# Feed-forward first products of groups 1 to 3 as seven half-size products (Strassen-Winograd) instead of eight, with VectorE summing the weight tiles

## What the kernel computes

```python
def _squared_relu_mlp(x, w1, w2):      # w1: 1024 x 4096, w2: 4096 x 1024
    h = jax.nn.relu(x @ w1)
    return (h * h) @ w2
```

## Time and profile before

| | |
|---|---|
| median of three runs | 2035.89 us |
| the profiled execution: span, which is all that its record gives of its time | 2036.2 us |
| TensorE busy with matmuls | 2016.6 us (99%), clock granted in full |
| VectorE busy | 1043.6 us (51%) |
| ScalarE busy | 803.1 us (39%) |
| DMA | 182.14 MB, 89 GB/s on average |

### The profile page before, as it was taken

The page is one execution under the profiler, slowest core; times in us unless marked ns, Lnnn a source line. Parts: engine busy times, 40 slices in busy tenths (PEclk is TensorE's granted clock), DMA queues, the critical chain, the costliest instruction groups (busy, mean ns, idle before and its releaser), DMA issues.

```text
span 2036.2 us, 27767 instructions
## 1 busy us (share of the span) xinstructions
PE 2016.6 (99%) x11212; PEld 1707.4 (84%) x11212; DVE 1043.6 (51%) x1722; ACT 803.1 (39%) x1354; POOL 174.5 (9%) x162
## 2 busy tenths in 40 slices
PE   9999999999999999999999999999999999999998
PEld 7888898888889888889888888987888898888887
DVE  6657777344345636537443434738544545334344
ACT  6425654232233533324332323535544345223232
POOL 1001010100002002210210003300000220000000
PEclk9999999999999999999999999999999999999999
DMA  5222012232322322222323223232122313332321
GB/s 189 83 73 74 22 53 92 95 104 92 103 83 94 124 93 83 83 94 83 104 86 111 82 93 104 94 104 94 53 63 83 99 52 98 103 104 84 112 83 52
DMA packets 52002, 182.14 MB, mean 89 GB/s; under 512 B 5824, under 2 KB 8016, under 8 KB 51888
## 3 DMA queue, kind: packets, MB, share of 16 engines
q1 hardware_dynamic: 50064, 173.23, 26.6%
q0 software_dynamic: 1824, 7.32, 1.1%
HBM read 178.43 MB, written 2.10 MB: 89 GB/s over the span
## 4 chain that ended last, share of the span: by engine, by line
PE 93%; DVE 3%; ACT 2%; issue 1%; DMA 1%; POOL 0%; SPq 0%; ACTq 0%; DVEq 0%
PE ps L411 60%; PE ps L1126 5%; PE ps L492 4%; PE ps L531 3%; PE ps L1789 3%; PE ps L1866 3%; PE ps L1066 2%; PE ps L1109 2%; PE ps L1083 1%; PE ps L1488 1%; PE ps L1879 1%; PE ps L847 1%; PE ps L1625 1%; PE ps L1777 1%; PE ps L1833 1%; PE ps L1743 1%
## 5 line engine op out<-in xcount | busy, mean ns | idle before, releaser
L411 PE MATMUL ps<-xa,ring 128*128 128x512 f32 x3048 | 702.6, 391 | 0.0
L411 PEld LDWEIGHTS ps<-xa,ring 128*128 128x128 f32 x3048 | 570.4, 188 | 119.6 <-issue 2.0
L411 PE MATMUL ps<-xb,ring 128*128 128x512 f32 x2208 | 502.6, 389 | 0.0
L411 PEld LDWEIGHTS ps<-xb,ring 128*128 128x128 f32 x2208 | 414.5, 188 | 86.0
L384 DVE TENSOR_TENSOR ring<-raw,ring 128x1024 fp32r<-128x1024 f32 x320 | 403.8, 1267 | 161.5 <-ACT ring L376 160.7
L376 ACT ACTIVATE ring<-raw 128x1024 fp32r<-128x1024 f32 x320 | 334.9, 1053 | 300.3 <-DMA raw<-in_stream 300.2
L989 DVE TENSOR_TENSOR acc<-acc,ps 128x512 f32<-128x512 f32 x68 | 46.8, 688 | 222.5 <-PE ps L411 222.5
L972 DVE TENSOR_TENSOR ffsq<-relu 128x512 f32<-128x512 f32 x96 | 66.4, 692 | 181.7 <-ACT relu L931 181.7
L931 ACT ACTIVATE relu<-ps 128x512 f32<-128x512 f32 x64 | 38.2, 596 | 227.7 <-PE ps L411 225.4
L975 DVE TENSOR_TENSOR xb<-ffsq,xb 128x512 fp32r<-128x512 f32 x96 | 66.5, 693 | 75.8 <-ACT xb L923 75.8
L1126 PE MATMUL ps<-xa,ring 128*128 128x512 f32 x432 | 104.3, 396 | 0.0
(11 more groups left out here) (368 smaller groups left out, 2055.5 us busy)
## 6 DMA issues: line engine op xcount, KB each, us to landing
raw<-in_stream SPq DMA_DIRECT2D x320, 512.0 KB, 3.5
t<-in_rpb POOLq DMA_DIRECT2D x8, 384.0 KB, 4.8
h<-in_x SPq DMA_DIRECT2D x8, 256.0 KB, 6.8
c_w<-in_cmp_w POOLq DMA_DIRECT2D x4, 512.0 KB, 4.7
out_y<-h SPq DMA_DIRECT2D x10, 128.0 KB, 1.9
out_y<-h SPq DMA_DIRECT2D x3, 256.0 KB, 2.2
cons<-in_con SPq DMA_DIRECT2D x1, 578.0 KB, 8.8
raw<-in_stream SPq DMA_DIRECT2D x2, 256.0 KB, 3.9
```

The lines of the kernel that those rows point to most:

```text
L411: mm = nc.tensor.matmul(bank[:, :], ring[:, slot_of(n, looped), w, k * P:(k + 1) * P], operand[:, k, xx], start=(start and i == 0 and w == ...
```

## The change

Let a 1024x1024 part of w1 act on all 512 tokens. It is cut in two halves of 512 hidden channels (u = 0, 1). In each half the weights are a 2x2 arrangement of tiles ("11", "12", "21", "22": rows are output channels, columns input channels, each tile 256 outputs by 512 inputs, stored as 128x1024), and the input is a 2x2 arrangement of 512 channels by 256 tokens. Eight products of tile by quarter become seven (Winograd's form of Strassen's method): the tile used is sometimes a sum of tiles, and the quarter used is sometimes a mix of quarters. One product is 2 x 4 blocks x 3 matmuls, 24 matmuls of 256 columns.

What is done for it, in groups 1 to 3 of each feed-forward:

- TensorE: `pe_set`, seven products for each half, 336 matmuls of 256 columns a group. Five PSUM results are combined, two accumulate into earlier banks.
- VectorE: four sums of weight tiles (128x1024, `dve_add_tile`) for each half before the split, seven splits, five sums of 128x512 results (`dve_set_sums`, `dve_set_22`, `dve_set_12`, `dve_set_21`) and four low parts (`dve_quad_lo`). It no longer squares the relu.
- ScalarE: seven splits for each half, a copy out of PSUM (`act_set_a`), and for each of four quarters a relu and two squares (`act_quad`; with a bias the relu is two instructions).
- DMA: seven landings for each half (the four tiles, some of them loaded twice) and one more of tile "21" into `other`.
- Splits run two products ahead inside the sets, three before them.
- The first panel of the second product takes its blocks in the order (0,1), (4,5), (2,3), (6,7), each pair after its own low parts.
- Once per feed-forward, in the second product of group 0: four mixes of quarters (`dve_mixed_raw`, 16 VectorE instructions of 128x256), their high parts on ScalarE, their low parts on VectorE (4 of 128x1024), and four ScalarE copies of 128x256. The squares of `h` move to panels 7 to 10, two a panel.
- The hardware loops are written out. The means' matmuls move from the head of the last group into group 2, `pool_base_sum` runs before `pool_squares(pool, 2)`, and several semaphores are shared (a semaphore's name and count change, not what waits for what).
- Two VectorE instructions of 128x8 near the start of the kernel make `minus`, the negated gains.

The core of the diff:

```diff
+SET_LANDS = ("11", "22", "11", "12", "11", "12", "22")
+SET_ADDS = (None, "21", 1, 2, "21", None, None)
+SET_SUM = (None, 1, 2, 3, 4, None, None)
+SET_TURN = (0, 1, 2, 4, 3, 5, 6)
+SET_BANK = (0, 2, 1, 3, 1, 0, 3)
...
         def dve_split(dve, n):
             m = n + AHEAD
...
+            if m + 1 < NP and summed(m + 1) is not None:
+                dve_add_tile(dve, m + 1)
+            dve.wait_ge(hi_done, m + 1)
+            at = set_of(m)
+            if at is not None and at[1] in SET_ADDS:
+                dve.wait_ge(sem("set_sums"), summed(m + 1))
             nc.vector.tensor_tensor(ring[:, at_slot, 1], raw[:, at_slot, 1], ring[:, at_slot, 0].bitcast(F32),
                                     ALU.subtract).then_inc(lo_done, 1)
...
+        def dve_add_tile(dve, n):
+            d, i = set_of(n)
+            dve.wait_ge(landed[n % RING], 16 * (n // RING + 1))
+            if SET_ADDS[i] == "21":
+                dve.wait_ge(sem(f"other_in{d % 2}"), 16 * (d // 2 + 1))
+                more = other[:, d % 2]
+            else:
+                dve.wait_ge(sem("set_sums"), summed(n - i + SET_ADDS[i]))
+                more = raw[:, SLOT[n - i + SET_ADDS[i]], 1]
+            nc.vector.tensor_tensor(raw[:, SLOT[n], 1], raw[:, SLOT[n], 1], more, ALU.add).then_inc(sem("set_sums"), 1)
...
+        def pe_set(pe, s, g, u):
+            first, d = set_at(s, g, u)
+            for c in range(SEVEN):
+                n = first + SET_TURN[c]
+                bank = ps[BANK[n]]
+                if c < 4:
+                    pe_free_bank(pe, BANK[n], first)
...
+                if c == 4:
+                    pe.wait_ge(sem("set_sum"), 5 * d + 1)
+                if c == 5:
+                    pe.wait_ge(sem("set_act"), 9 * d + 1)
+                if c == 6:
+                    pe.wait_ge(sem("set_sum"), 5 * d + 3)
+                pe.wait_ge(lo_done, n + 1)
+                moving = set_moving(c)
+                for i in range(2):
+                    for k in range(4):
+                        for w, xx in ((0, 0), (0, 1), (1, 0)):
+                            at_w = (4 * i + k) * P
+                            mm = nc.tensor.matmul(bank[:, half(i)], ring[:, SLOT[n], w, at_w:at_w + P], moving[:, k, xx],
+                                                  start=(c < 5 and i == 0 and k == 0 and w == 0 and xx == 0),
+                                                  stop=(i == 1 and k == 3 and w == 1),
+                                                  skip_group_check=c >= 5)
+                mm.then_inc(panel_done, 1)
...
+            for g in range(1, GROUPS):
+                pe_set(pe, s, g, 0)
+                pe_set(pe, s, g, 1)
+                for k in range(KC if g < GROUPS - 1 else KC - 4):
+                    n = base + second_of(g) + k
+                    if k == 0:
+                        for i, (pair, quads_in) in enumerate((((0, 1), 3), ((4, 5), 4), ((2, 3), 7), ((6, 7), 8))):
+                            pe.wait_ge(sem("ff_lo"), u0 + KC * g + quads_in)
+                            pe_panel(pe, n, xb, blocks=pair, free=i == 0, split=i == 0, start=i == 0, stop=i == 3, last=i == 3)
...
+        def ffn_splits(s, g, j):
+            n = BASE[s] + first_of(g) + j
+            if g == 0:
+                ahead = (3,) if j >= 4 else ()
+            elif j < 2 * SEVEN:
+                ahead = (2,) if j > 0 else ()
+            else:
+                ahead = ((2,), (2, 3))[j - 2 * SEVEN] if j < 2 * SEVEN + 2 else (3,)
...
+            for g in range(1, GROUPS):
+                for u in range(2):
+                    for c in range(SEVEN):
+                        if c == 0 and u == 1:
+                            dve_set_21(dve, s, g, 0)
+                            dve_quad_lo(dve, s, g, 0, "11")
+                        if c == 3:
+                            dve_set_sums(dve, s, g, u)
+                        if c == 4:
+                            dve_set_22(dve, s, g, u)
+                        if c == 5:
+                            dve_set_12(dve, s, g, u)
+                        split(g, SEVEN * u + c)
+                        if c == 1 and u == 1:
+                            dve_quad_lo(dve, s, g, 0, "21")
+                        if c == 5:
+                            dve_quad_lo(dve, s, g, u, "22")
+                        if c == 6:
+                            dve_quad_lo(dve, s, g, u, "12")
...
-            with dve.Fori(1, 3) as g:
...
+            pool_base_sum(pool)
             pool_squares(pool, 2)
-            pool_base_sum(pool)
```

More of the change, by code:

```diff
@@ L274, in build @@
         bqa = keep("bqa", [P, 4])
+        minus = keep("minus", [P, 2, KC])
         shared = place[0] + (P - place[0]) % 256
@@ L397, in pe_free, with pe_panel @@
                 pe_free_bank(pe, bank, n, more)
-        def pe_panel(pe, n, operand, ready=None, more=0, free_more=0, blocks=range(KC), bank=None, free=True,
-                     last=True, start=True, stop=True, split=True, looped=False):
+        def pe_panel(pe, n, operand, ready=None, blocks=range(KC), bank=None, free=True,
+                     last=True, start=True, stop=True, split=True):
             if free:
-                pe_free(pe, n, free_more)
+                pe_free(pe, n)
             if split:
-                pe.wait_ge(lo_done, n + 1 + more)
+                pe.wait_ge(lo_done, n + 1)
             bank = ps[BANK[n]] if bank is None else bank
@@ L905, in pe_ffn @@
[L905 to L910, removed]
-                        pe_base_mean(pe)
-                pe_panel(pe, base + 6 * KC + j, xa if j < KC else xb, (sem("ff_lo"), u0 + 3 * KC) if j == KC else None)
-            pe_tail(pe, s, xb, tail, inside)
+            for g in range(1, GROUPS):
[7 more added lines that the diff above has]
+                            pe_panel(pe, n, xb, blocks=pair, free=i == 0, split=i == 0, start=i == 0, stop=i == 3, last=i == 3)
+                    else:
+                        pe_panel(pe, n, xb)
+                    if k == 0 and g == GROUPS - 2 and squares is not None:
+                        pe_squares(pe, squares)
+                        if s == "ffn1":
+                            pe_base_mean(pe)
@@ L940, in act_ffn @@
                         .then_inc(sem("acc_begun"), 1)
-                if squares is not None and j >= KC:
-                    act_square(act, squares, j - KC, h[:, j - KC])
-            with act.Fori(1, 3) as g:
-                for j in range(2 * KC):
-                    act_split(act, base + j, more=64 * g, looped=True)
-                    panel(g, j)
-            for j in range(2 * KC - 4):
-                act_split(act, base + 6 * KC + j)
-                if squares is not None and j == 2:
-                    act.wait_ge(sem("x_summed"), squares + 1)
-                    nc.scalar.activation(part[:, :], ps[7][:, :], ACT.Square, scale=ROOT8, bias=con_col("eps8"))\
-                        .then_inc(sem("base_ready"), 1)
-                panel(3, j)
-                if r is not None and j > KC:
-                    post_full(act, s, r, j - KC - 1)
@@ L957, in act_ffn @@
+            split(GROUPS - 1, LATER - 4)
             if r is not None:
@@ L990, in gather @@
                 ins.then_inc(taken["dve"], 1)
-            first, last = 0, 3
             for j in range(2 * KC):
-                if j >= 4:
-                    dve_split(dve, base + j)
+                split(0, j)
                 if j < KC:
-                    square(first, j)
+                    square(j)
                 else:
-                    gather(first, j)
-            with dve.Fori(1, 3) as g:
-                for j in range(2 * KC):
-                    dve_split(dve, base + j, more=2 * KC * g, looped=True)
-                    if j < KC:
-                        square(g, j)
-                    else:
-                        gather(g, j)
@@ L1007, in dve_ffn @@
-            for j in range(2 * KC - 4):
-                dve_split(dve, base + 6 * KC + j)
-                if j < KC:
-                    square(last, j)
-                else:
-                    gather(last, j)
-                if s == "ffn1" and 2 <= j < 2 + KC:
-                    dve_base_centre(dve, j - 2)
-            dve_split(dve, base + 7 * KC + 4)
+                    gather(0, j - KC)
+                i = j - KC
+                if 0 <= i < 4:
+                    dve_mixed_raw(dve, s, i)
```

380 lines of the change are left out of this document (290 added, 90 removed).

## The result

The changed kernel takes 2012.06 us (median of four runs, 2011.64 to 2014.28) against 2036.11 us: a ratio of 0.9884, 95% interval 0.987 to 0.9898. 2011 was forecast, in a range of 2006.5 to 2022.

A forecast was written before the change was run, and what follows sets the result against it. TensorE, busy 99% of the span, was taken as the bound. 2036.2 - 29.1 (saving) + 3.6 (stall) + 0.5 (once-only work) = 2011.2 us, 2010.9 for the median, stated as 2011; range 2006.5 to 2022.

The forecast's parts named there:

- TensorE's saving: In the sets, 336 matmuls at 119.9 ns replace 192 at 226.7: 3.24 us less a group, 29.1 in nine.
- stall at turn 3 of the second half: Fourth product of a set's second half: TensorE waits for VectorE's split, 0.4 us a group, 3.6 in nine.
- once-only work: Mixes, moved squares, start-up instructions and the base sum, done outside the sets: nearly all covered, 0.5 us together.
- base sum: GpSimd's sum right after the boundary in ffn1: covered by the three panels of lead of VectorE's splits, 0 to 0.5 us.
- hand-over to the second product: After a set, low part "21" comes before TensorE wants it: nothing lost, half a microsecond spare, about 0.3 in ffn2.
- VectorE is busy 18.0 of 20.14 us in a half: In each half of a set, VectorE's instructions back to back nearly fill TensorE's time: 18.0 of 20.14 us.
- a gap before turn 3 and none elsewhere: Profile after the change: TensorE waits only before the fourth product of a set's second half, until VectorE's split ends.
- B: Inside the sets VectorE is the bound, waits undoing its overlap: 1.6 us a group or more, 2016 to 2027; chance 0.18.
- C: In the sets VectorE's instructions take 1.3 times their time, from GpSimd or unseen cause: 5.5 us a group, 2057; chance 0.06.
- D: In long stretches of 256 columns matmuls run slower; at 129.6 ns nothing is saved, 2036 us; chance 0.06.
- E: In the sets' second halves tiles land late, up to 2 us a group: 2016 to 2029 us; chance 0.08.

The follow-up runs named there:

- e9: The changed kernel with the last product of each half multiplied twice, so eight half-size products: 2061.56 us.
- e2: The changed kernel with VectorE's low part of quarter 21 made one turn later, behind the split of tile 4: 2011.76 us.
- e4: The changed kernel with VectorE's sums of weight tiles done on 8 columns in place of 1024, waits kept: 2009.72 us.
- e5: The changed kernel with one more VectorE sum of 128x1024 in each half, before the sum that makes tile 4: 2022.67 us.
- e1: The changed kernel with GpSimd's base sum moved back behind its squares: 2010.36 us.
- after_again: The changed kernel measured again with no edit: 2012.28 us.
- e7: The changed kernel with three more tiles that nobody reads loaded in each half of a set in ffn2: 2012.56 us.
- e6: The changed kernel with 14 GpSimd sums of 128x512 beside the sets in each of groups 1 to 3 of ffn0 alone: 2055.35 us.

## Why the prediction was right

| step | predicted us | measured us |
|---|---|---|
| TensorE's saving, nine groups | -29.1 | 9 x (40.31 - 43.52) = -28.9 |
| stall at turn 3 of the second half | +3.6 (0.4 each) | 9 x (40.58 - 40.31) = +2.4 |
| once-only work | +0.5, at most 0.5 of it the base sum | +2.5, the base sum in ffn1 |
| hand-over to the second product | 0 | +0.5 in ffn2, +0.2 in the other six groups |
| sum | -25.0 | -23.3, where -23.4 is measured from ffn0 on |

The sum leaves 0.1 us, so the loops written out and the means' matmuls moved give and cost nothing that shows.

*TensorE's saving* was right, by the row of L492: the pitch held through stretches of 336 matmuls, and e9 shows that a product costs its 2.88 us.

*The stall* was right in place and cause, and a third smaller than forecast (0.27 us a group, not 0.4): in ffn0's group 1 the product began 0.08 us late, where I had reckoned 0.22. e2 and e4 remove the stall in two ways and both leave 40.31 us; e5 adds 1.14 us to the list and the sets grow by 1.13. That VectorE is busy 18.0 of 20.14 us in a half was wrong as a mean: it is 31.3 in the 40.6 us of both halves, since three splits and three sums of the first half are done in the panels before, and two low parts and a sum of results come behind the sets. The argument went by the list of the second half and did not rest on the mean.

*The base sum* is the mis-sized term. The step "covered by their three panels of lead, 0 to 0.5" failed twice. First, the only price that the prediction had for GpSimd beside VectorE was a median of 1.59 us for a split, a factor of 1.3, from a stretch where GpSimd's sums of 1.3 us come one by one with 2 to 4 us between most of them. The base sum runs without a pause, and there a split takes 2.3 us and a square 1.77. The trace of before had a row of this: the same base sum, at 1014.6 to 1026.9 in ffn1, and a split of 2.05 us beside it:

```profile
L384 DVE TENSOR_TENSOR ring<-raw,ring x3: 1216/1590/2053, 1013.7 to 1024.6; 128x1024 fp32r<-128x1024 f32 x3
```

Second, I gave VectorE the lead of the splits, but its list there also holds the squares and low parts of four panels at once, which TensorE wants in the first panel of the second product. e1 gives the 2.5 us back. The prediction's sign "a gap before turn 3 and none elsewhere" failed here as well.

*The hand-over* had a margin of "about 0.3" in ffn2 by my count. In groups 1 and 2 that was right: the last low part was there 3.72 us after the sets, TensorE wanted it at 4.08, and the second products lost 0.05 us each (43.57 against 43.52). In the last group it came at 4.09, and some 0.4 us were lost:

```profile
1945.87 0.69 DVE L1095 TENSOR_TENSOR xb<-quads,xb 128x512 fp32r<-128x512 f32 x1 [0.94 <-ACT quads L1088]
```

ScalarE's last square had ended at 1945.42, as early after the sets as in the other groups, and VectorE began 0.45 us later instead of 0.1. It did so in after_again, e1, e4 and e7 too; the cause stays open. In e2 ScalarE itself was late, and 0.36 us went in groups 1 and 2 as well.

*The rivals.* B is out by e4. What C assumes, VectorE slower beside GpSimd, was there in e6 and stronger than I priced it: 14 us a group, with GpSimd at work without a pause, against 5.5, enough to turn the sign. But GpSimd is idle in the sets, 0.00 in the windows. D is out by the pitch. E is out by e7 up to 247 GB/s; a full load was not tried.

*Luck.* The sum is closer than its terms: the stall was 1.2 us too dear, the base sum and the hand-over 2.7 us too cheap, and 1.6 us are left between -25.0 and -23.4. In the medians 24.05 us were gained; the 0.65 us more than in the part compared are scatter, most likely of the start-up.

## What to carry to other kernels

Where TensorE is 99% busy, look for the start-to-start distance of the cheaper form in a stretch of the same form, which may be in the trace already: 119.9 ns in L492's stretch here, and 119.97 in the 336 matmuls of e4. 12.5% fewer columns became 7.4% less time; by my estimate from the two distances (2 x 119.9 less 226.7) 13 ns of a matmul did not shrink with its columns. For what the change loads on another engine, a busy share doesn't decide (VectorE was busy 31.3 of 40.6 us, and TensorE still waited for it); write down that engine's list between the last signal it waits for and the first thing that is wanted of it, with start-to-start distances, and compare the two times. Keep GpSimd's work out of the stretches where VectorE's list is on the path (14 us a group in e6), and take its price from rows with full overlap (2.2 to 2.3 us for a split here, not the 1.59 of the row with pauses); and when a wait is removed, look for what it was hiding (0.36 us a group in ffn2 in e2).

## What was not expected of the hardware

In e6, beside GpSimd sums without pauses, VectorE's instructions with two inputs in SBUF took 0.9 to 1.0 us more each in both sizes that ran there: 2.22 us in place of 1.22 for a 128x1024 split, 1.6 in place of 0.69 for a 128x512 low part, so 1.8 and 2.3 times as long. Four of 128x512 with an input in PSUM ran in the same 28 us and stayed at 0.68 to 0.69:

```profile
L1116 DVE TENSOR_TENSOR quads<-quads,ps 128x512 f32<-128x512 f32 x1 | 0.7, 686 | 1.1 <-PE ps L1009 1.1
L1105 DVE TENSOR_TENSOR quads<-quads,ps 128x512 f32<-128x512 f32 x1 | 0.7, 686 | 0.0
L1121 DVE TENSOR_TENSOR quads<-ps,quads 128x512 f32<-128x512 f32 x1 | 0.7, 678 | 0.0
L1103 DVE TENSOR_TENSOR quads<-quads,ps 128x512 f32<-128x512 f32 x1 | 0.7, 675 | 0.0
```

The clock granted to TensorE fell below 1.00 in e6. Six windows in the sets of one group, two of them inside others; the column before the DMA share is the granted clock:

```profile
399.10:410.00 10.90, 8.58 (x72) 8.37 (x70) 10.80 (x7) 6.07 (x9) 10.48 (x6) 1.00 0.59 195
410.00:418.00 8.00, 3.26 (x25) 3.12 (x26) 7.89 (x6) 2.84 (x4) 7.69 (x5) 0.86 0.21 77
418.00:426.20 8.20, 5.06 (x25) 4.88 (x25) 8.20 (x5) 3.34 (x4) 7.89 (x5) 0.71 0.20 64
426.20:439.35 13.15, 13.15 (x97) 13.15 (x98) 8.42 (x10) 7.83 (x13) 0.98 (x1) 0.88 0.37 121
...
417.85:423.05 5.20, 5.19 (x24) 4.98 (x24) 5.20 (x3) 1.06 (x1) 5.04 (x3) 0.55 0.00 0
426.18:428.00 1.82, 1.82 (x8) 1.82 (x9) 1.79 (x3) 0.23 (x1) 1.00 (x1) 0.50 0.00 0
```

TensorE had waited 2.4, 4.7 and 3.1 us for splits, and was busy 3.26 us of the second window's 8.00. A product of 24 matmuls in the third took 5.20 us in place of 2.88, at a granted clock of 0.55; after the third wait the first 8 matmuls ran at 0.50. From 430.70 on the grant is 1.00 again. The last 96 matmuls of the sets took 13.16 us. In the changed kernel the same 96 take 11.75, also behind a wait (0.26 us without weight loads) but at 1.00. So some 1.4 of the 14 us a group are the clock's; the product of 5.20 us cost nothing more, since the chain was on VectorE at that time. In e6 the third wait, of 3.1 us, cost 1.4 us beyond its length. The low grants stand behind the waits, but no run here varied their length, so what brings them down was not shown.
